# The samples' value rows copied to all partitions by DMA from a scratch in DRAM instead of by one-hot matmuls

## What is computed

```python
z = _rmsnorm(h, g_mix) @ w_in            # q, f, i (values), out gate, conv value, conv gate
fgate = lb + (1.0 - lb) * sigmoid(f)
k, v = 1.0 - fgate, i                    # per head
# a sample has one token, so for each of 16 samples and 8 heads:
S_new = fgate[:, None] * S0 + k[:, None] * v[None, :]     # 128 x 128, f32 state
o = S_new^T @ silu(q)
# group B: GLU, causal depthwise convolution of width 31, group norm, silu
h = h + concat(o_a, o_b) @ w_out
h = h + (silu(hf @ w_gate) * (hf @ w_up)) @ w_down
```

## Time and profile before

| | us |
|---|---|
| median of 3 runs | 1734.06 (1733.07 to 1734.46) |
| the profiled execution's own time | 1737.78 |
| its span (core 0, the slowest of 8) | 1736.2 |
| spans of the 8 cores | 1724.9 to 1736.2 |
| TensorE busy | 1655.8 (95%) |
| VectorE busy | 523.1 (30%) |
| ScalarE busy | 518.4 (30%) |
| GpSimd busy | 151.2 (9%) |

### The profile page before, as it was taken

How to read it: one execution, slowest core, us unless ns; L and a number is a source line. 1 busy time by engine, 2 the same in 40 slices (tenths; PEclk the granted TensorE clock), 3 DMA queues, 4 the chain that set the end, 5 groups by cost and what they waited for, 6 DMA issues and landing times.

```text
span 1736.2 us, 31827 instructions; the slowest of 8 cores (1724.9 to 1736.2 us)
## 1 busy us (share of the span) xinstructions
PE 1655.8 (95%) x13252; PEld 1165.2 (67%) x13252; DVE 523.1 (30%) x949; ACT 518.4 (30%) x979; POOL 151.2 (9%) x112
## 2 busy tenths in 40 slices
PE   3789999999899999999999999999999999999998
PEld 3566677676566554446666666666666688888887
DVE  3226836476754444442111111111111101010106
ACT  3355636576655666111010001000100010110102
POOL 1010111111312000001010010101010000000000
PEclk9799999999999999999999999999999999999999
DMA  9659555758669966339573738465564365666665
GB/s 204 167 112 174 94 73 77 142 91 146 131 135 183 243 137 119 134 127 158 74 98 49 98 51 140 65 82 76 72 85 62 49 115 93 92 92 92 92 117 206
DMA packets 266795, 197.22 MB, mean 114 GB/s; under 512 B 3707, under 2 KB 254971, under 8 KB 262319
## 3 DMA queue, kind: packets, MB, share of 16 engines
q0 software_dynamic: 210304, 111.15, 49.6%
q1 hardware_dynamic: 39421, 74.60, 13.7%
q10 hardware_dynamic: 16928, 9.44, 2.0%
HBM read 271.57 MB, written 28.04 MB: 173 GB/s over the span
## 4 chain that ended last, share of the span: by engine, by line
PE 87%; DMA 4%; DVE 3%; ACT 3%; issue 2%; DVEq 0%; POOL 0%; ACTq 0%; SPq 0%; POOLq 0%
PE PS L668 50%; PE PS L1362 18%; PE PS L1217 6%; DMA arena<-w_in 3%; PE PS L588 3%; PE PS L527 3%; PE PS L751 2%; PE PS L1038 1%; PE PS L470 1%; DMA arena<-xall 1%; PE PS L1384 1%; DMA scn<-arena 0%; PE PS L912 0%; DVE arena L691 0%; DVE arena L921 0%
## 5 line engine op out<-in xcount | busy, mean ns | idle before, releaser
L668 PE MATMUL PS<-arena 128*128 128x344 bf16 (+4 forms) x6144 | 923.7, 311 | 0.9 <-ACT arena L990 0.5
L668 PEld LDWEIGHTS PS<-arena 128*128 128x128 bf16 x6144 | 596.9, 98 | 306.9 <-issue 4.0
L1362 PE MATMUL PS<-arena 128*128 128x256 bf16 x2816 | 310.4, 273 | 0.0
L1362 PEld LDWEIGHTS PS<-arena 128*128 128x128 bf16 x2816 | 274.8, 98 | 34.5 <-issue 1.7
L1318 DVE TENSOR_TENSOR arena<-PS,arena 128x352 bf16<-128x352 f32 (+1 forms) x132 | 68.5, 519 | 544.5 <-PE PS L668 543.9
L1316 ACT ACTIVATE arena<-PS 128x352 f32<-128x352 f32 (+1 forms) x132 | 60.7, 459 | 554.4 <-PE PS L668 554.4
L1217 PE MATMUL PS<-arena 128*128 128x512 bf16 x512 | 113.1, 379 | 2.0 <-ACT arena L1063 1.7
L1371 ACT ACTIVATE arena<-arena 128x256 bf16<-128x256 f32 x64 | 26.7, 417 | 274.5 <-DVE arena L1369 274.4
L1369 DVE TENSOR_TENSOR arena<-PS,arena 128x256 f32<-128x256 f32 x64 | 27.1, 424 | 253.9 <-PE PS L1362 240.9
L1217 PEld LDWEIGHTS PS<-arena 128*128 128x128 bf16 x512 | 49.6, 98 | 60.8 <-issue 3.4
L347 POOL DMA_DIRECT2D arena<-w_gate x22 | 25.1, 1142 | 690.8 <-PE PS L668 492.8
(11 more groups left out here) (167 smaller groups left out, 1101.1 us busy)
## 6 DMA issues: line engine op xcount, KB each, us to landing
arena<-w_in POOLq DMA_DIRECT2D x32, 1024.0 KB, 12.6
arena<-xall SPq DMA_DIRECT2D x24, 1024.0 KB, 8.3
arena<-w_gate POOLq DMA_DIRECT2D x22, 1024.0 KB, 9.5
arena<-w_up POOLq DMA_DIRECT2D x22, 1024.0 KB, 12.3
arena<-w_down POOLq DMA_DIRECT2D x8, 2816.0 KB, 22.4
arena<-arena SPq DMA_DIRECT2D x32, 263.0 KB, 7.1
arena<-sh SPq DMA_DIRECT2D x16, 512.0 KB, 4.8
shn<-arena ACTq DMA_DIRECT2D x16, 512.0 KB, 4.7
```

Source lines behind the costliest of these rows:

```text
L668: ins = e.matmul(ps(b)[:, 0:n], wv[:, k, m * 128:(m + 1) * 128], src3[:, k, c0:c0 + n], start=(k == 0), stop=(k == 15))
L1362: ins = e.matmul(ps(b)[:, 0:256], hm3[:, k, ti * 128:ti * 128 + 128], wv[:, k, :], start=(k == 0), stop=(k == NFF - 1))
```

## The change

The value rows of the samples are written once to a scratch `vsd` in DRAM, in the order head, sample, value. Each group of 8 samples of a head then gets a tile of 128 x 1024 bf16 by one transfer whose source has a step of 0 over the partitions (128 reads of the same 2 KB). Two tiles are used in turn, at places where the prefix's values `Vp` lay before. VectorE's multiply-add reads this tile in place of PSUM. The one-hot matrix, its making and the 128 matmuls are gone, and the multiply-adds no longer use the bank in `MISC`.

```diff
+    vsd = dt("vsd", [8, 16, 128], BF).ap()
...
-        oneh = T(9480, 1024)
-        oneh3 = oneh.b.rearrange("p (s m) -> p s m", m=128)
+        vb_ = [T(42504, 512), T(43016, 512)]
...
-        op("dve", lambda e: e.tensor_copy(
-            out=oneh3[0:32], in_=cst.f[0:32, C_ID + 16:C_ID + 32].unsqueeze(2).to_broadcast([32, 16, 128])),
-            [cst.r], [oneh.r], cost=2.0)
+        dma("sp", vsd.rearrange("h s v -> s h v"), VS.b[16:32, :].rearrange("s (h v) -> s h v", v=128),
+            rd=[VS.s(i) for i in range(4)], wr=[P.named("vsd")], key="vsd", nb=33e3)
...
+                vbt = vb_[gi % 2]
+                vb3 = vbt.b.rearrange("p (s v) -> p s v", v=128)
+
+                def vload(e, sem, vbt=vbt, h=h, s0=s0):
+                    v = vsd[h, s0:s0 + 8].rearrange("s v -> (s v)")
+                    e.dma_start(out=vbt.b, in_=bass.AP(v.tensor, v.offset, [(0, 128), (1, 1024)])).then_inc(sem, 16)
+                op("sp", vload, [P.named("vsd")], [vbt.r], cost=.4, key="vb%d" % (gi % 2), nb=262e3, ndma=1)
...
                 for hf in range(2):
-                    b = nxt("misc", MISC)
-                    v3 = ps(b).rearrange("p (s v) -> p s v", v=128)
-
-                    def vb(e, v3=v3, hf=hf, h=h, s0=s0):
-                        ins = None
-                        for s in range(4):
-                            ins = e.matmul(v3[:, s, :], oneh3[0:32, s0 + hf * 4 + s, :], VS.b[0:32, h * 128:(h + 1) * 128],
-                                           start=True, stop=True)
-                        return ins
-                    op("pe", vb, [oneh.r, VS.s(gp)], px=[b], cost=.4)
-
-                    def upd(e, v3=v3, hf=hf, m=m, s0=s0, S03=S03):
+                    def upd(e, vb3=vb3, hf=hf, m=m, s0=s0, S03=S03):
...
-                                out=S03[:, ss, :], in0=v3[:, s, :],
+                                out=S03[:, ss, :], in0=vb3[:, ss, :],
...
-                    op("dve", upd, [fks.s(m), S0.r], [S0.r], px=[b], cost=1.4)
+                    op("dve", upd, [fks.s(m), S0.r, vbt.r], [S0.r], cost=1.2)
```

## The result

The kernel after took 1752.16 us where the one before took 1734.26 (medians of 4 executions each): a ratio of 1.0097, 95% interval 1.0078 to 1.0117, so 17 us slower. One of the four after, at 1807.45 us, fell in a slower state of the chip, in which the granted clock is lower; all ratios leave such executions out, and without it the median is 1751.47. The profiled execution took 1748.92 us against 1737.78, with a span of 1747.4 against 1736.2.

A forecast was written before the change was run, and what follows sets the result against it. It took TensorE, busy 95% of the span, as the bound, except at changes of head pairs, where VectorE and ScalarE end last. Terms -9 - 2 + 2 - 2 + 1.5 + 17 + 1.7 - 1.5 = +7.7 gave 1741 us, range 1723 to 1750.

The forecast's parts named there:

- The queue at the end of the stage: On GpSimd's queue, w_out's four loads precede w_in's last two, so TensorE waits at conv group 6: +17 us.
- its lower bound: At conv group 6, the eight loads at GpSimd's mean pace take 98 in place of 107.8 us, leaving +7.
- +2 (the first eight ahead of an eviction): After the prefix, the first value load and eight multiply-adds delay an eviction from 223.4 to 225.5 us: +2.
- -2 (fewer of them at the third change of heads): Between 406 and 445 us, VectorE has 16 multiply-adds where it had 24: -2 us.
- +1.5 (held beside GpSimd): VectorE's SBUF multiply-adds meet GpSimd's multiplications four or five times, a microsecond each, a third on the path: +1.5.
- The removed matmuls: In the samples' stretch, 128 one-hot matmuls in 32 calls, 10.5 us of TensorE's time, go: -9.
- 2 more for waits: TensorE's waits in front of the one-hot matmuls, 4.7 us, go as well, partly spent anyway: -2.
- The 7.6 us of the chain: The chain of waits goes through enough one-hot matmul calls to make 2.1% of 360 us: 7.6 us.
- The clock: After the gap at conv group 6, TensorE is granted its lower clock for a while: +1.7 us.
- their rival: Late value loads on SP delay state loads, GpSimd and w_in: +8, 1749; chance 0.15, shared with held ports.
- a sign of being wrong: VectorE waiting for the value transfers (arena<-vsd) more than 3 us in all would show the forecast wrong.
- the wait for a shift transfer: TensorE's 2.0 us wait at 575 us goes, since the new order spreads the convolution halves: -1.5.

The follow-up runs named there:

- e4: The kernel before with the last two loads of w_in moved behind all four of w_out in GpSimd's list; ratio 1.0109.
- e3: The kernel after with the order of the kernel before on every engine, each value load placed where its tile comes free; ratio 0.9978.
- e5: The kernel after with the multiply-adds recorded again as users of the one bank in MISC, no matmul added; ratio 1.0066.
- e11: e1 with a fourth tile for old states, same order on every engine, only the state loads issued earlier; ratio 1.0021.
- e1: The kernel after with the last two loads of w_out moved behind the last two of w_in in GpSimd's list; ratio 1.0034.
- e6: e5 with, besides, the last two loads of w_out moved behind the last two of w_in; ratio 0.9962.
- e8: The kernel before with each call of four one-hot matmuls issuing them twice, 256 in place of 128; ratio 1.0032.
- e7: The kernel before in its own order with the scratch write and 16 value loads added, read by nothing; ratio 0.9997.
- e12: The kernel after with four state tiles, everything placed anew by the scheduler, and w_out's last two loads behind w_in's; ratio 0.9972.
- e9: e3 with GpSimd's product of the states cut to one column of each state, the rest left undecayed; ratio 0.9955.

## Why the prediction was wrong

It said 1741 us, 1723 to 1750, most likely slower. The sign was right, and so was the mechanism of its largest term. The time was 1752, outside the range, because a second loss of the same size stood in the sum at next to nothing.

**The queue at the end of the stage: right, and over-sized in one figure.** The wait on w_in came at the first projection of group 6, in all cores, 9.7 to 13.1 us in place of 17. In core 2, counted from the start of group 2 at 523.3 us: TensorE was done with the convolution ahead of group 6 at 603.2 (614.59 - 11.38), +80, where the prediction had +83.5. The first slab landed at 614.5 (559.8 + 54.7), the second at 619.7 (562.2 + 57.5), +96, against 103. The second was needed at +82.5, so the queue cost 14 us there, 12.1 of waits and 1.6 of lower clock. The eight loads took 99 us in all, from the first issue at 520.25 to the last landing; the prediction had 107.8 by the landings of before and, for its lower bound, 98 by the mean pace of GpSimd's queue, which was the better figure (with 5 us taken off either, it had landings at +103 and +93). On the kernel before, where nothing else moved, the same order cost 11.4 to 17.1 us of wait and 19 us in all (e4), which is the 17 and 1.7 of the sum (17.4 us by the mean of the cores).

**The step that failed is the price of the new places on VectorE.** The prediction looked at where the multiply-adds had moved to and gave this +2 (the first eight ahead of an eviction), -2 (fewer of them at the third change of heads) and +1.5 (held beside GpSimd). It asked what they would hold up while they ran, and never what they would wait for. TensorE's waits on VectorE rose by 11.0 us (8.6 to 19.6). Before, each multiply-add came after a one-hot matmul that had to take its turn on the bank, and VectorE's rows on waiting for it (13.4 us in core 0) never became one on GpSimd. With that tie gone the scheduler put them where they come up directly behind GpSimd's product. (That it reckoned the state loads to land too early is likely, but no run shows it.) In the run that load waits for one of three tiles, and VectorE's list is in order. The warning was in the rows: GpSimd waited 107.4 us for state loads, and the prediction used this row to argue that such waits reach nobody. That was so only while VectorE had other work in front of the multiply-adds. The evidence is of three kinds: the same work in the old order has 9.0 us of TensorE's waits on VectorE (e3), the tie alone brings them to 2.6 (e5), and a fourth state tile, with only the state loads moved, removes most of the idle time on the product (e11). The price at the end is less sharp than the 11 us of waits, since waits on ScalarE grow where those on VectorE fall (20.6 in e5): e1 to e6 says 7.7 us in the mean of the cores and 12 in the time.

**A term that was not in the sum: the cores drift apart.** The prediction added up one core and took the others to be alike. The slowest lay 7.9 us above the mean after the change, and 11.0 in e1, where it had been about 5. The time is that of the slowest core, so this adds some 3 to 6 us; the ties between these and the late product are seen in e1 and e11 (above), and not tested further.

**The removed matmuls: busy time right, worth over-sized.** TensorE's busy time fell by 10 us (417.7 to 407.7 in e1, where no clock is lost to the gap at group 6), and the term counted 9 of it, and 2 more for waits. Doubling them costs 5.5 us in the timed runs (e8), and removing them in an unchanged order gives 3.8 (e3). The 7.6 us of the chain were nearer. The first table's first column puts them at 8.6 and 3.9, the mean of the cores at 6.2 and 4.1, so this size is known only to within a factor of two. Here luck comes in: this term and the queue's were over-sized by some 5 us each, with opposite signs, and cancelled in the sum.

**The clock: under-sized.** At the gap it is the 1.6 us that the projection at 614.59 took over, as said (1.7). But there were four more such places, where TensorE had waited 2.3 to 4.8 us for VectorE (at the last of them before had one too); four windows of 10 us from 240 us on show it (the columns are those of the earlier trace rows):

```profile
240.00:250.00 10.00, 7.36 (x51) 4.60 (x50) 6.67 (x19) 5.13 (x8) 3.04 (x2) 0.96 0.82 181
320.00:330.00 10.00, 7.70 (x59) 4.96 (x58) 5.20 (x14) 7.04 (x12) 3.05 (x2) 0.88 0.53 91
410.00:420.00 10.00, 5.36 (x41) 3.77 (x40) 5.04 (x14) 1.16 (x3) 3.06 (x2) 0.82 0.87 137
470.00:480.00 10.00, 6.86 (x42) 4.47 (x43) 5.15 (x9) 2.20 (x6) 1.56 (x2) 0.66 1.23 203
```

After and e1 differ by 3.4 us in TensorE's busy time for the same matmuls (411.1 and 407.7). That is what the lower clock took beyond e1, which still has the stalls of VectorE; the granted clock from 220 to 650 us was 0.96 after, 0.98 in e1 and 0.99 before, in the slowest core of each.

**Right:** the value transfers are hidden (e7; their rival is out, except that the first one came 3.3 us late in core 2 and up to 3.7 in others, just over the 3 us that the prediction named as a sign of being wrong, and within its term of +2, bounds 0 and 5), the multiply-add itself is as long from SBUF as from PSUM (medians of 345 and 342 ns), the wait for a shift transfer is gone, and everything from the output projection on takes as long as before (1076.2 us to the end of the span, against 1075.7).

**VectorE held beside GpSimd: about as priced.** In the kernel after it is one place a core: in core 2, at 468.0 us, eight multiply-adds took 4.39 us in place of 2.38, beside a product from 469.12 to 471.45, and TensorE then waited 4.77 us for VectorE, so up to 2.0 us for the +1.5 of the sum. In the old order there are four to six places, as the four or five that were estimated, nearly all held longer than the microsecond that was allowed. (The row of 6.31 us from which the prediction starts lay beside two products, from 463.10 to 465.46 and from 465.42 to 467.31, not one.) The Trainium skill (SBUF — State Buffer, section SBUF: two separate sides) says that an operation of VectorE with two SBUF inputs and one of GpSimd that reads SBUF exclude each other for the whole instruction; e3's timeline agrees, as the hold ends with the product.

**The sum again, from the medians:** -10.0 (matmuls) + 3.4 (clock) + 11.3 (w_in) + 11.0 (VectorE) - 2.5 (ScalarE) - 2.7 (the shift transfer) = 10.5, of 12.1 in the first column. The forecast, set against the profiled execution of before, was 7.7. The timed runs show 17; part of the difference is that the slowest core counts and now lies further from the others, part that the profiled execution of before lay 3.7 us above its median and that of after was the lowest of its four.

## What to carry to other kernels

When work is taken out of a kernel whose order is made by a list scheduler, list what the removed operations had kept apart, and look, for every operation that moves up, at what it now waits for and at what stands behind it on its engine; a wait that cost nothing behind other work can reach the end when it stands at the head of a list (here 41.7 us of one engine's idle time became 11 us of another's waits). A queue that lands its loads in order is priced by adding up the bytes from the point where the first buffer comes free; here the mean pace over the span gave 98 us for loads that took 99. Test an edit in the old order first: here the same change is 1% slower as scheduled, 0.2% faster in the old order (e3) and 0.4% faster with the tie and w_in ahead (e6), by nothing but places. And look at the spread of the cores beside the median: e1's typical core was as fast as before, and its slowest 6 us slower.

## What was not expected of the hardware

A single small transfer can be late by itself: of the 16 value loads of 256 KB, with a median of 5 to 8 us from issue to landing in each core, the slowest took 13 to 18 us in six cores of e11 and up to 28.0 in one of e12, where it was at most 9.9 in the kernel after, without any change in what they move. And a gap of TensorE is paid twice: after the 11.4 us without work, 16 matmuls of 358 columns took 4.15 us in place of 2.59, at a granted clock of 0.62. And the hold of VectorE by GpSimd is exact: in the eight cores of after, e1, e3, e5, e6, e9 and e12 there are 164 multiply-adds of over 0.4 us (the median is 0.35), and each ends 0.14 to 0.16 us after a product of GpSimd; 14 of them had started 0.15 to 1.1 us before the product, while GpSimd was still issuing a load. With one operand in PSUM, in before, none of 1024 took over 0.352.
